# Two layers of windowed attention: value products issued for four units at a time, with five buffers for the turned probabilities

## The reference

```python
BLOCK = WINDOW = 128                       # 8 query heads of 64, 2 key heads, 256 context rows
def one_block(args):                       # for each 128 rows of queries, with context and window
    s_loc = jnp.where(valid, einsum('bqkgd,bnkd->bkgqn', qi, ks), -inf)
    s_ctx = einsum('bqkgd,bnkd->bkgqn', qi, kc)
    p = sink_softmax(concatenate([s_ctx, s_loc]), sink_b)
    return p[..., :nc] @ vc + p[..., nc:] @ vs
def context_attention(q, k, v, sink_b):    # first layer only: the 256 context rows among themselves
    ...
a = window_attention(q, k, v, kc, vc, sink_b)
h = concatenate([a * silu(ga), f * silu(gf), s * silu(gc)]) ; y = h @ w_out
```

## Time and profile before

| | |
|---|---|
| median of 3 runs | 1861.59 us (1860.95 to 1862.58) |
| the profiled execution | 1860.51 us, its span 1858.7 us |
| TensorE matmuls busy | 1830.9 us, 99% of the span |
| ScalarE, VectorE, GpSimd busy | 802.7, 771.7, 790.6 us |
| mean granted clock of TensorE | 0.998 of full speed |

### The profile page before, as it was taken

One profiled execution on the slowest core, in us unless ns is written; L12 is line 12 of the kernel. 1 busy time (PEld: TensorE's weight loads), 2 busy tenths in 40 slices (PEclk: granted clock), 3 DMA queues, 4 the chain that ended last, 5 costly groups with the idle time before them and its releaser, 6 DMA issues.

```text
span 1858.7 us, 26490 instructions
## 1 busy us (share of the span) xinstructions
PE 1830.9 (99%) x10358; PEld 1532.0 (82%) x10358; DVE 771.7 (42%) x1679; ACT 802.7 (43%) x1571; POOL 790.6 (43%) x639
## 2 busy tenths in 40 slices
PE   8999999999999999999999999999999999999997
PEld 6888887888887888768888888888876898888886
DVE  4575575376473454876111110065377621111003
ACT  5222386472376565872323222127488233222213
POOL 2433372265553453334444444435322444444442
PEclk9999999999999999999999999999999999999999
DMA  9554412124402243103333333223310333333321
GB/s 331 195 151 152 131 46 69 57 91 141 138 24 71 71 139 95 58 25 91 91 110 95 91 94 133 87 87 108 118 47 19 94 102 100 91 91 113 114 91 45
DMA packets 195242, 185.60 MB, mean 100 GB/s; under 512 B 24150, under 2 KB 162564, under 8 KB 195120
## 3 DMA queue, kind: packets, MB, share of 16 engines
q1 hardware_dynamic: 180520, 172.51, 29.4%
q10 hardware_dynamic: 14600, 11.41, 2.2%
HBM read 179.11 MB, written 5.44 MB: 99 GB/s over the span
## 4 chain that ended last, share of the span: by engine, by line
PE 89%; ACT 4%; POOL 2%; DVE 2%; issue 1%; SPq 1%; DMA 1%; DVEq 0%; ACTq 0%; POOLq 0%
PE ps L1536 25%; PE ps L1538 25%; PE ps L1537 25%; PE ps L2079 3%; PE ps L2196 2%; PE ps L2175 2%; POOL w_lo L833 1%; PE ps L1598 1%; PE ps L1615 1%; PE ps L1631 1%; PE ps L2171 1%; ACT pt L1026 1%; ACT w_hi L968 1%; ACT sc L1016 1%; PE ps L1557 1%
## 5 line engine op out<-in xcount | busy, mean ns | idle before, releaser
L833 POOL TENSOR_TENSOR w_lo<-raw,w_hi 128x512 fp32r<-128x512 f32 (+1 forms) x505 | 671.0, 1360 | 828.3 <-ACT w_hi L968 828.1
L968 ACT ACTIVATE w_hi<-raw 128x1024 fp32r<-128x1024 f32 (+1 forms) x273 | 255.2, 980 | 262.6 <-PE ps L1538 190.9
L1536 PE MATMUL ps<-g_hi,w_lo 128*128 128x512 f32 (+1 forms) x928 | 348.4, 375 | 0.7 <-POOL w_lo L833 0.7
L1537 PE MATMUL ps<-g_lo,w_hi 128*128 128x512 f32 (+1 forms) x928 | 347.4, 374 | 0.0
L1538 PE MATMUL ps<-g_hi,w_hi 128*128 128x512 f32 (+1 forms) x928 | 347.4, 374 | 0.0
L1536 PEld LDWEIGHTS ps<-g_hi,w_lo 128*128 128x128 f32 x928 | 174.7, 188 | 33.0 <-POOL w_lo L833 1.1
L1537 PEld LDWEIGHTS ps<-g_lo,w_hi 128*128 128x128 f32 x928 | 174.7, 188 | 31.1
L1538 PEld LDWEIGHTS ps<-g_hi,w_hi 128*128 128x128 f32 x928 | 174.7, 188 | 31.0
L2940 DVE TENSOR_TENSOR tmp_f<-ps,tmp_f 128x512 f32<-128x512 f32 x44 | 30.4, 692 | 370.0 <-PE ps L1538 370.0
L1536 PE MATMUL ps<-h_hi,w_lo 128*128 128x512 f32 (+1 forms) x496 | 176.9, 357 | 0.1
L1537 PE MATMUL ps<-h_lo,w_hi 128*128 128x512 f32 (+1 forms) x496 | 174.6, 352 | 0.0
(11 more groups left out here) (305 smaller groups left out, 3229.6 us busy)
## 6 DMA issues: line engine op xcount, KB each, us to landing
raw<-in_w_in SPq DMA_DIRECT2D x33, 1024.0 KB, 5.1
raw<-in_w_mod SPq DMA_DIRECT2D x24, 1024.0 KB, 6.6
raw<-in_w_gate SPq DMA_DIRECT2D x44, 512.0 KB, 3.8
raw<-in_w_up SPq DMA_DIRECT2D x44, 512.0 KB, 4.9
raw<-in_w_down SPq DMA_DIRECT2D x22, 1024.0 KB, 4.8
raw<-in_w_out SPq DMA_DIRECT2D x8, 1024.0 KB, 5.0
strips<-bias_rows ACTq DMA_DIRECT2D x18, 256.0 KB, 4.1
raw<-in_w_o SPq DMA_DIRECT2D x4, 1024.0 KB, 4.9
```

The lines of the kernel that those rows point to most:

```text
L833: pool.tensor_tensor(w_lo[:, i % SPLIT, a:e], raw_of(what)[:, a:e], w_hi[:, i % SPLIT, a:e].bitcast(F32), ALU.subtract).then_inc(s_tile_lo ...
L968: act.activation(w_hi[:, i % SPLIT, a:b], raw_of(what)[:, a:b], ACT.Copy).then_inc(s_tile_hi.sem, s_tile_hi.nth((what, n)))
L1536: pe.matmul(o, lhs[1], rhs[0], start=first, stop=False)
L1537: pe.matmul(o, lhs[0], rhs[1], start=False, stop=False)
```

## The change

The second layer from unit 0, and the first layer from unit 24 (pair 12) on, issue their value products for four units at a time. An even pair k is deferred: its mix moves from step k+1 to step k+2, right ahead of the mix of pair k+1. Even steps so hold two mixes, between their two turns, and odd steps none. The two pairs write different 128 columns of bank 7. VectorE takes the rows of a pair one step later, and for a deferred pair it waits for the mixes of both. The buffers for turned units become five: in the first layer two more over the tile cb, in the second two over the Fourier tables (there is a single added wait on ScalarE, for unit 24 of the first layer, on the last side input that GpSimd makes from cb and gf). The banks of the turns and the waits on them stay as they are.

```diff
--- before.py
+++ after.py
@@ -222,6 +222,9 @@
         sc = at("sc", [P, 4, 5 * P + 8], names["h_hi"][0])
         pt = [at("pt0", [P, 5 * P], names["h_lo"][0]), at("pt1", [P, 5 * P], names["h_lo"][0] + 4 * 5 * P),
               at("pt2", [P, 5 * P], names["mod_row"][0] + names["mod_row"][1] - 4 * 5 * P)]
+        pt_cb = [at(f"pt_cb{i}", [P, 5 * P], names["cb"][0] + 4 * 5 * P * i) for i in range(2)]
+        pt_dft = [at(f"pt_dft{i}", [P, 4 * P], names["dft_ccos"][0] + 4 * 4 * P * i) for i in range(2)]
+        assert 2 * 4 * 5 * P <= names["cb"][1] and names["dft_ccos"][0] + 2 * 4 * 4 * P <= names["pt2"][0]
         assert names["mod_row"][0] == names["wf_m"][0] + names["wf_m"][1] and names["wf_m"][1] + names["mod_row"][1] >= 4 * 5 * P
         k_twice = [at("k_twice0", [P, TOK], names["cz"][0] + 4 * TOK, F32R),
                    at("k_twice1", [P, TOK], names["h_lo"][0] + 4 * 2 * 5 * P, F32R)]
@@ -733,6 +736,24 @@
 
         TURN_BANK, OUT_BANK = 4, 7
 
+        BY_FOUR = (24, 0)
+
+        def deferred1(y, k):
+            return 2 * k >= BY_FOUR[y] and k % 2 == 0
+
+        def pt_slot(y, r):
+            if r < BY_FOUR[y]:
+                return pt[r % 3]
+            if y == 0:
+                return (pt + pt_cb)[r % 5]
+            return pt_dft[r // 4 % 2] if r % 4 == 0 else pt[r % 4 - 1]
+
+        def used_last(y, r):
+            for one in range(r - 1, -1, -1):
+                if pt_slot(y, one) is pt_slot(y, r):
+                    return one // 2
+            return None
+
         def turn_at1(units, r):
 
             n = len(units[r]["vs"])
@@ -1021,9 +1042,11 @@
                     n = P * len(units[r]["vs"])
                     o0 = turn_at1(units, r)
                     act.wait_ge(s_turned.sem, s_turned.at((y, r)))
-                    if r >= 3:
-                        act.wait_ge(s_mixed.sem, s_mixed.at((y, (r - 3) // 2)))
-                    act.activation(pt[r % 3][:, 0:n], ps_flat[:, o0:o0 + n], ACT.Copy).then_inc(s_pt.sem, s_pt.nth((y, r)))
+                    if used_last(y, r) is not None:
+                        act.wait_ge(s_mixed.sem, s_mixed.at((y, used_last(y, r))))
+                    if r == BY_FOUR[0] and y == 0:
+                        act.wait_ge(s_side_lo.sem, s_side_lo.at((y, 3)))
+                    act.activation(pt_slot(y, r)[:, 0:n], ps_flat[:, o0:o0 + n], ACT.Copy).then_inc(s_pt.sem, s_pt.nth((y, r)))
                     if EARLY1 <= r + 2 < len(units):
                         exp1(y, units, r + 2)
                     at_step(r + EARLY1 - 1)
@@ -1621,14 +1644,15 @@
                     n = len(two[0]["vs"])
                     assert n == len(two[1]["vs"])
                     pe.wait_ge(s_pt.sem, s_pt.at((y, 2 * k + 1)))
+                    o = P * (k % 2)
                     if k == 0:
                         pe.wait_ge(*emptied[OUT_BANK])
-                    else:
+                    elif not deferred1(y, k - 1):
                         pe.wait_ge(s_o_out.sem, s_o_out.at((y, 2 * k - 1)))
                     for j in range(n):
                         for half in range(2):
                             own = slice(HD * half, HD * half + HD)
-                            m = pe.matmul(ps[own, OUT_BANK, 0:P], two[half]["vs"][j], pt[(2 * k + half) % 3][:, P * j:P * j + P],
+                            m = pe.matmul(ps[own, OUT_BANK, o:o + P], two[half]["vs"][j], pt_slot(y, 2 * k + half)[:, P * j:P * j + P],
                                           start=j == 0, stop=j == n - 1)
                     m.then_inc(s_mixed.sem, s_mixed.nth((y, k)))
 
@@ -1636,7 +1660,9 @@
                 for k in range(last + 1):
                     if k < last:
                         turn(2 * k)
-                    if k > 0:
+                    if k > 1 and deferred1(y, k - 2):
+                        mix(k - 2)
+                    if k > 0 and not deferred1(y, k - 1):
                         mix(k - 1)
                     if k < last:
                         turn(2 * k + 1)
@@ -2338,17 +2364,20 @@
 
                 def rows_out(k):
 
-                    dve.wait_ge(s_mixed.sem, s_mixed.at((y, k)))
+                    dve.wait_ge(s_mixed.sem, s_mixed.at((y, k + 1 if deferred1(y, k) else k)))
+                    o = P * (k % 2)
                     for half in range(2):
                         u, own = units[2 * k + half], slice(HD * half, HD * half + HD)
-                        V.tensor_tensor(u["out"], ps[own, OUT_BANK, 0:P], u["gate"], ALU.mult).then_inc(s_o_out.sem, s_o_out.nth((y, 2 * k + half)))
+                        V.tensor_tensor(u["out"], ps[own, OUT_BANK, o:o + P], u["gate"], ALU.mult).then_inc(s_o_out.sem, s_o_out.nth((y, 2 * k + half)))
 
                 for i in range(EARLY1):
                     scored(i)
                     first(i)
                 last = len(units) // 2
                 for k in range(-1, last + 1):
-                    if k >= 1:
+                    if k >= 2 and (deferred1(y, k - 2) or deferred1(y, k - 3)):
+                        rows_out(k - 2)
+                    if k >= 1 and not deferred1(y, k - 1) and (not deferred1(y, k - 2) or k == last):
                         rows_out(k - 1)
                     for i in (2 * k + EARLY1, 2 * k + EARLY1 + 1):
                         if EARLY1 <= i < len(units):
```

## The result

The kernel after takes 1868.17 us (median of 6 runs, 1867.53 to 1870.0) against 1861.37 us (6 runs, 1860.87 to 1862.64) before: 1.0037 times, 95% interval 1.0024 to 1.0050. It is slower by 6.8 us, where 6.9 us were forecast. The profiled execution takes 1867.53 us with a span of 1865.7 us, 7.0 us more than before.

What follows compares the result with a forecast made beforehand. TensorE bounds the second layer, TensorE and ScalarE in turns the first. +5.0 (second) and +1.9 (first) make +6.9 on 1860.51, 1867.4, and with 1.1 for the median 1868.5 us; range 1863.0 to 1872.0.

Steps and rivals of the forecast that it cites:

- Odd step of width 5: Second layer, without its mix: odd turn starts 1.59 us after the even one, not 1.66; TensorE stands 1.07 us.
- Even step: Second layer: takes the 16 records of the pair of width 4 without a trip of their own, +0.87 us.
- Second layer: Its attention, summed over groups of four units: +5.0 us, bounds 3.7 to 6.1.
- the two with weight splits: Second layer's groups from units 20 and 24: +0.80 us, and +0.53 us where ScalarE also splits weights.
- First layer: Its attention from unit 24, summed over steps: +1.9 us, bounds 0 to +3.
- step 17: First layer, width 2: loses 20 records and a trip, 1.36 us, but scores wait for VectorE's masks; -1.1 us.
- the end: End of the first layer: pairs 22 and 23 go together, last 8 records at 310.35; -0.3 us.
- What costs nothing: Five buffers, the wait before unit 24, VectorE's later reading, DMA and queues: no added time.
- The trip: TensorE changing from turns into a mix and out again: 0.27 us each, 14 removed, 3.8 us if issue alone decided.
- the trips decide and the copy stays hidden: Rival at odd turns of width 5: faster, 1857.8 us without a stall, 1856.3 by the drain rule; chance 0.08.
- later waits take it up: Rival in both layers: no change, first layer gives nothing, second half of 3.7, +1.9 us, 1863.5 us; chance 0.12.
- ScalarE too late in every odd step: Rival: slower still, ScalarE's 0.25 us slack and 0.3 more gone in 10 odd steps, +3.0, 1871.4 us; chance 0.07.

Runs made afterwards that it cites:

- mix_behind: Kernel before, but in the second layer's odd steps the mix stands behind the second turn, nothing deferred, five buffers: 1868.73 us, 1.0044 against before.
- banks_after: Changed kernel with odd turned units starting in bank 6, so fewer blocks share a bank with the even unit: 1864.14 us, 1.0015 against before.
- odd_deferred: Change in the second layer only, but deferring odd pairs instead of even ones; first layer keeps its order: 1862.28 us, 1.0007 against before.
- scores_between: Change in the second layer only, odd turned units in bank 6, next scores between the two turns of odd steps: 1859.84 us, 0.9995 against before.
- banks_before: Kernel before, order and buffers kept, with odd turned units starting in bank 6: 1858.71 us, 0.9989 against before.
- buffers_only: Changed kernel's five buffers, halves of bank 7 and added wait, but the order of mixes as before: 1860.86 us, 1.0000 against before.
- more_trips: Kernel before with seven more round trips: second layer's even steps 2 to 14 cut the mix around the second turn: 1862.61 us, 1.0009 against before.
- banks_late: Kernel before with odd turned units from unit 3 on in bank 6, unit 1 still in bank 5: 1858.38 us, 0.9986 against before.
- first_only: The change in the first layer alone (from unit 24), second layer as before: 1863.81 us, 1.0017 against before.
- second_only: The change in the second layer alone, first layer as before: 1866.30 us, 1.0031 against before.

## Why the prediction was right

The sum held step by step. The step lengths after, less those before:

- **Odd step of width 5:** forecast 1.59 us from turn to turn with TensorE standing; measured 1.59 to 1.60 in the second layer. mix_behind shows it without any batching, banks_after nearly halves it, odd_deferred and scores_between cover it.
- **Even step:** forecast +0.87, measured 2.64 against 1.77, +0.87.
- **Second layer:** forecast +5.0, measured +4.98. Four groups grew by 0.76 us each on average (0.80 forecast), the two with weight splits by 0.87 and 0.59 (0.80 and 0.53), the rest by 0.60 (0.5), the first group, with its one odd step, by -0.09 (-0.07).
- **First layer:** forecast +1.9, measured +1.94. Step 14 +0.87 (0.87); steps 15 and 16 +0.26 (0.3); step 17 -1.17 (-1.1); steps 18 and 19 +0.97 (0.92); step 20 +0.87; steps 21 and 22 +0.26 (0.3); the end -0.1 (-0.3), the one term that was clearly off. These lengths fit, but no experiment separates their causes, and banks_after against banks_before shows that the cost here does not come from the shared banks.
- **What costs nothing:** buffers_only shows it, 0.0 us. One reason given was wrong: a buffer is not used again two steps after its mix, but in part in the same step (unit 5 takes unit 1's, whose mix stands in step 2 just ahead of the turn of unit 5). The copy waits for a turn behind that mix in any case, and in the change no copy of either attention has idle time that a mix ended.
- **Later waits take nothing up:** the lengths sum to +6.9 us, and the span grew by 7.0.

The trip was priced too low: 0.27 us forecast, 0.33 as a mean in more_trips, and 6.68 + 1.07 - 7.43 = 0.32 us in the change itself. That is most of why a group grew by 0.76 us and not by 0.80: the odd turn, with no mix ahead of it, takes 545.77 - 545.28 = 0.49 us up to its scores, where the forecast kept 0.52. The miss stayed small because the forecast added up step lengths, in which the price of a trip enters little. Of the rivals, "the trips decide and the copy stays hidden" falls by the 1.59 us, "later waits take it up" by the second layer's full 4.98 us, and "ScalarE too late in every odd step" by 1.59 us there too; it is late only in the two groups with splits, where TensorE stands 1.20 us by the brackets.

## What to carry to other kernels

A piece of work that stands between two steps may be covering a wait that no profile row shows, because it is covered: before moving it, work out when the next step could start without it. Where work is batched, place the long piece between the two steps that share a resource (here two turns in one bank), not wherever the counting starts. And a wait in which the copy does come late says where buffers are short: putting half of the turned units in an idle bank gained more than any order, 0.35 us in a head of the first layer and 0.28 us in each of the second layer's two groups with weight splits. Where the mix covered the copy, it gained nothing (6.67 to 6.72 us a group in banks_late).

## What was not expected of the hardware

- TensorE's granted clock fell to 0.50 for 3.4 us after it stood for 1.68 us (first_only, 281.8 to 285.2), and that made the attention 1.44 us longer. After the same stall in another execution of the same order it didn't fall. The stalls of 1.1 us in the second layer were in no profiled execution followed by one.
- Falls of the same 3.4 us stand near the start of four other profiled executions (second_only from 21.6, odd_deferred from 21.7, banks_before from 21.3, banks_late from 22.3), each at the end of a stretch of 2.4 to 2.6 us in which TensorE stood for a weight tile, or up to 1.1 us behind it; in scores_between and banks_after it stood there 2.4 and 2.8 us and the clock didn't fall. These four executions took 0.7 to 1.6 us longer than the medians of their kernels, so such falls may be part of the scatter of whole times. The row of second_only:

```profile
21.57:24.98 3.41, 3.41 (x21) 2.05 (x14) 0.44 (x1) 0.38 (x1) 2.80 (x2) 0.50 1.04 410
```

- In a mix at half the clock two records took 0.21 us instead of 0.11, so the fall shows in the spacing of starts as well as in the clock.
